# Value products spread over the projection, and page transfers in another order, in a one-core decoder step

## The reference

```python
h = _rmsnorm(x, pre_w)
z = h @ w_in                                  # 2048 -> 6980 columns
qa, ka, va, ga, qs, ks, vs, gs, qi, ki, wi = _split_cols(z)
# group A: differential attention, 8 heads
pr = softmax(s1) - lam * softmax(s2)
oa = einsum('bhqs,bshd->bqhd', pr, va_all)    # sample rows: 32 pages of keys and values each
# group B: the 256 best keys of each row by an indexer score
_, idx = lax.top_k(score, topk)
x = x + _rmsnorm(concat(oa, ob) @ w_out, post_w)
x = x + sigmoid(x @ w_pg + b_pg) * (p @ w_pe)
```

## Time and profile before

| | us |
|---|---|
| median of 3 runs | 3952.08 |
| lowest, highest | 3949.98, 3962.9 |
| the profiled execution, its own time | 3954.57 |
| its span in the trace | 3952.8 |
| TensorE busy in the span | 3453.9 (87%) |
| mean granted TensorE clock | 0.927 of full |
| DMA, mean over the span | 126 GB/s |

### The profile page before, as it was taken

One profiled execution on the slowest core, in us unless ns is written; L12 is line 12 of the kernel. 1 busy time (PEld: TensorE's weight loads), 2 busy tenths in 40 slices (PEclk: granted clock), 3 DMA queues, 4 the chain that ended last, 5 costly groups with the idle time before them and its releaser, 6 DMA issues. The chain is left out here.

```text
span 3952.8 us, 46957 instructions
## 1 busy us (share of the span) xinstructions
PE 3453.9 (87%) x16995; PEld 2339.6 (59%) x17025; DVE 1497.0 (38%) x2771; ACT 820.3 (21%) x1798; POOL 514.0 (13%) x480
## 2 busy tenths in 40 slices
PE   4969789898988888889358699999979999899999
PEld 3757567676766666667223677777744444444443
DVE  2028666666666676654555111111110002311111
ACT  4011424141423333221000122222220001110000
POOL 0004333333333232310000200000000000000000
PEclk9989899998999999999669699999989999999999
DMA  9864676666666766754100211111041101310110
GB/s 341 253 192 145 189 259 195 226 213 223 222 224 217 226 224 200 242 163 135 53 0 9 77 27 28 27 28 27 10 156 43 43 22 53 113 59 32 59 59 22
DMA packets 344067, 497.51 MB, mean 126 GB/s; under 512 B 58913, under 2 KB 244538, under 8 KB 342674
## 3 DMA queue, kind: packets, MB, share of 16 engines
q1 hardware_dynamic: 338384, 481.67, 38.3%
q10 hardware_dynamic: 3922, 8.65, 0.6%
q0 software_dynamic: 1536, 4.20, 0.4%
HBM read 466.55 MB, written 27.90 MB: 125 GB/s over the span
## 5 line engine op out<-in xcount | busy, mean ns | idle before, releaser
L1244 PE MATMUL Z<-W,hT 128*128 128x256 f32 x4608 | 1063.8, 389 | 37.7 <-ACT qk L829 24.1
L1244 PEld LDWEIGHTS Z<-W,hT 128*128 128x128 f32 x4608 | 887.7, 196 | 165.3 <-ACT qk L829 26.5
L2138 PE MATMUL S<-W,hT 128*128 128x512 f32 x1408 | 646.1, 597 | 8.1 <-DMA hT<-oT_d 8.1
L2138 PEld LDWEIGHTS S<-W,hT 128*128 128x128 f32 x1408 | 264.9, 191 | 356.0 <-issue 346.9
L800 POOL TENSOR_TENSOR kprod<-kib,qib 128x256 f32<-128x256 f32 x256 | 231.5, 908 | 696.8 <-DVE srel L965 554.2
L962 DVE TENSOR_REDUCE sc<-big 128x16 f32<-128x1024 f32 x256 | 309.7, 1210 | 0.5 <-DVE isc L999 0.3
L2138 PE MATMUL Z<-W,hT 128*128 128x512 f32 x640 | 303.6, 592 | 0.0
L794 POOL TENSOR_TENSOR big<-big,qb 128x1024 f32<-128x1024 f32 x96 | 231.9, 2416 | 274.6 <-DMA big<-in_cache_diff_k_dram 274.6
L1316 PE MATMUL DB<-big,ex 128*4 128x256 f32 (+1 forms) x2112 | 150.7, 397 | 109.1 <-DMA big<-in_cache_diff_v_dram 108.9
L958 DVE TENSOR_TENSOR big<-big,qb 128x1024 f32<-128x1024 f32 x160 | 197.6, 1235 | 126.4 <-DMA big<-in_cache_diff_k_dram 123.5
L2138 PEld LDWEIGHTS Z<-W,hT 128*128 128x128 f32 x640 | 121.5, 190 | 153.0 <-issue 152.6
(11 more groups left out here) (539 smaller groups left out, 3305.5 us busy)
## 6 DMA issues: line engine op xcount, KB each, us to landing
big<-in_cache_diff_k_dram SPq DMA_DIRECT2D x256, 512.0 KB, 5.5
big<-in_cache_diff_v_dram SPq DMA_DIRECT2D x256, 512.0 KB, 5.0
W<-in_w_in_dram SPq DMA_DIRECT2D x27, 2048.0 KB, 10.0
W<-in_w_in_dram SPq DMA_DIRECT2D x52, 1024.0 KB, 7.3
W<-in_w_ple_gate_dram SPq DMA_DIRECT2D x16, 1024.0 KB, 5.1
W<-in_w_out_dram SPq DMA_DIRECT2D x12, 1024.0 KB, 5.1
kib<-in_cache_idx_k_dram SPq DMA_DIRECT2D x256, 32.0 KB, 2.3
hT<-oT_d SPq DMA_DIRECT2D x3, 2048.0 KB, 21.5
```

Of the source, the lines that this page charges most:

```text
L1244: mm = pe.matmul(Z[b][:, 0:CW], hT[:, k, t * P:(t + 1) * P], W[:, w, k, :], start=(k == 0), stop=(k == KT - 1))
L2138: mm = pe.matmul(b, hT[:, k, t * P:(t + 1) * P], Wr[:, k, :], start=(k == 0), stop=(k == KT - 1))
```

## The change

The value products get four positions per place instead of three, with one page behind each half and two at the end of a place. The transfers of a slot are sorted by the place at which a table expects their home to be free (`key_done`, `value_done`); weights and the store of the keys are inserted where the table passes 4.1 and 5.6. The two rounds of slot 0 move to slot 8, where `settle` moves to place 3 and each `select` two places later, the last two behind place 7. `turned(0)` moves ahead of `take(0, 15)`. The values' store of the last slot has a semaphore of its own, and `stage` waits for an earlier store.

```diff
-        VALUES = ((0, 0, 0), (0, 0, 4), (2, 0, 3), (2, 0, 3), (0, 2, 3), (0, 2, 3), (0, 2, 3), (0, 2, 1))
-        ROUNDS_IN = (2,) + (4,) * (HA - 1) + (1,)
+        VALUES = ((0, 0, 0, 0), (0, 0, 0, 2)) + ((1, 1, 1, 2),) * 6
+        key_done = lambda s: [t + (0.35 if n == 0 else 0.5 + 0.5 * n / PAGES[s][t]) for t in range(NT) for n in range(PAGES[s][t])]
+        value_done = [t + 0.25 * (q + 1) for t in range(NT) for q in range(4) for n in range(VALUES[t][q])]
+        def transfers(s):
+            keys = [(u, 0, p + 4) for p, u in enumerate(key_done(s)) if p + 4 < NPG] if s < HA else []
+            vals = [(u, 1, v + 3) for v, u in enumerate(value_done) if v + 3 <= NPG] if s else []
+            return sorted(keys + vals)
+        ROUNDS_IN = (0,) + (4,) * (HA - 1) + (3,)
...
-                    for i in range(NPG):
-                        if s < HA:
-                            if i % 4 == 0 and i + 4 < NPG:
-                                index_pages(s, i // 4 + 1)
-                            if i + 4 < NPG:
-                                key_page(s, i + 4)
-                        if s and i + 3 <= NPG:
-                            value_page(s - 1, i + 3)
-                        if i == 18 and s + 1 < SLOTS:
-                            weights(s + 1, 0)
-                        if i == 25:
-                            store_keys(s)
+                    due = [(4.1, lambda: weights(s + 1, 0))] if s + 1 < SLOTS else []
+                    due.append((5.6, lambda: store_keys(s)))
+                    for u, kind, n in transfers(s):
+                        while due and due[0][0] < u:
+                            due.pop(0)[1]()
+                        if kind == 0:
+                            if n % 4 == 0:
+                                index_pages(s, n // 4)
+                            key_page(s, n)
+                        else:
+                            value_page(s - 1, n)
+                    for _, late in due:
+                        late()
...
 def stage(s, f):   # ScalarE
+                    act.wait_ge(st_v, 16 * (h + 1))
...
 for c in range(2 * NT):   # ScalarE, slot 0
+                    if c == 2 * NT - 1:
+                        turned(0)
                     take(0, c)
...
-                    if c >= 2 * NT - ROUNDS_IN[0]:
-                        counts(0, c - 2 * NT + ROUNDS_IN[0])
-                turned(0)
...
-                for r in range(ROUNDS_IN[0]):   # VectorE
-                    update(r)
...
-                            if t == 1:
+                            if t == 3:
                                 settle()
-                            if t >= 2:
-                                select(t)
+                            if t >= 4:
+                                select(t - 2)
                             if t == NT - 1:
+                                select(NT - 2)
+                                select(NT - 1)
                                 dve.nop().then_inc(d_sel, 1)
...
 half(s, 2 * t, 0)   # TensorE
+                        v = some(s, v, VALUES[t][0])
 half(s, 2 * t, 1)
...
-                        for n in range(pre):
-                            values(s, v + n)
+                        v = some(s, v, VALUES[t][1])
...
-                            for n in range(mid):
-                                values(s, v + n)
+                        v = some(s, v, VALUES[t][2])   # at t >= 4 behind probabilities(s, t, 0)
...
-                        for n in range(post):
-                            values(s, v + n)
+                        v = some(s, v, VALUES[t][3])   # behind output(s, t)
```

More of the change, by code:

```diff
@@ L575, in hymba_step @@
         PAGES.update({s: (0, 5, 5, 6, 4, 4, 5, 3) for s in range(1, HA)})
-        VALUES = ((0, 0, 0), (0, 0, 4), (2, 0, 3), (2, 0, 3), (0, 2, 3), (0, 2, 3), (0, 2, 3), (0, 2, 1))
-        ROUNDS_IN = (2,) + (4,) * (HA - 1) + (1,)
+        VALUES = ((0, 0, 0, 0), (0, 0, 0, 2)) + ((1, 1, 1, 2),) * 6
+        assert sum(map(sum, VALUES)) == NPG
+        key_done = lambda s: [t + (0.35 if n == 0 else 0.5 + 0.5 * n / PAGES[s][t]) for t in range(NT) for n in range(PAGES[s][t])]
[5 more added lines that the diff above has]
+        ROUNDS_IN = (0,) + (4,) * (HA - 1) + (3,)
         FIRST_ROUND = [sum(ROUNDS_IN[:s]) for s in range(SLOTS + 1)]
@@ L661, in hymba_step @@
         d_sel = sem("a_dsel")
-        st_k, st_v, st_o = sem("a_stk"), sem("a_stv"), sem("a_sto")
+        st_k, st_v, st_sv, st_o = sem("a_stk"), sem("a_stv"), sem("a_stsv"), sem("a_sto")
         with nc.Block() as block:
@@ L726, in store_values @@
                             sp.dma_start(sv_p.rearrange("l b (t p) h d -> p (l b t) h d", p=P)[:, :, n, :],
-                                         vg[:, s % 2, n, :, :]).then_inc(st_v, 16)
+                                         vg[:, s % 2, n, :, :]).then_inc(st_sv, 16)
                 sp.dma_start(subw[:, :], sub_w.partition_broadcast(P).rearrange("q l d -> q (l d)")).then_inc(x_in, 16)
@@ L760, in _ @@
                         sp.dma_start(sc[0:1, NPG, :], snew_a_d[s:s + 1, :]).then_inc(row_in, 16)
-                    for i in range(NPG):
-                        if s < HA:
-                            if i % 4 == 0 and i + 4 < NPG:
-                                index_pages(s, i // 4 + 1)
-                            if i + 4 < NPG:
-                                key_page(s, i + 4)
-                        if s and i + 3 <= NPG:
-                            value_page(s - 1, i + 3)
-                        if i == 18 and s + 1 < SLOTS:
-                            weights(s + 1, 0)
-                        if i == 25:
-                            store_keys(s)
+                    due = [(4.1, lambda: weights(s + 1, 0))] if s + 1 < SLOTS else []
[11 more added lines that the diff above has]
+                        late()
                 store_values(SLOTS - 1)
                 sp.wait_ge(st_k, 16 * SLOTS)
-                sp.wait_ge(st_v, 16 * (SLOTS + 1))
+                sp.wait_ge(st_v, 16 * HA)
+                sp.wait_ge(st_sv, 16 * HKV)
             @block.gpsimd
@@ L1321, in values, with some @@
                         pe.nop().then_inc(db_full, 1)
+                def some(s, v, n):
+                    for q in range(n):
+                        values(s, v + q)
+                    return v + n
                 def columns(s):
@@ L1339, in _ @@
                     for t in range(NT):
-                        pre, mid, post = VALUES[t]
                         scores(s, t)
@@ L1350, in _ @@
                             pe.transpose(DB[0:16, 256:384], m16, ident[:, :]).then_inc(db_full, 1)
-                        for n in range(pre):
-                            values(s, v + n)
-                        v += pre
+                        v = some(s, v, VALUES[t][1])
                         if t < 4:
@@ L1369, in _ @@
                             probabilities(s, t, 0)
-                            for n in range(mid):
-                                values(s, v + n)
-                            v += mid
+                        v = some(s, v, VALUES[t][2])
+                        if t >= 4:
                             probabilities(s, t, 1)
@@ L1379, in _ @@
                         output(s, t)
-                        for n in range(post):
-                            values(s, v + n)
-                        v += post
+                        v = some(s, v, VALUES[t][3])
                     values(s, NPG)
```

## The result

The changed kernel takes 4013.01 us (median of 4 runs, 4009.94 to 4021.68) against 3951.67 for the kernel before on the same chip: a ratio of 1.0153, 95% interval 1.0128 to 1.0177. It is slower, by 61 us where 26.5 were forecast, and lies above the range (3890 to 4005). In the profiled execution the span is 4008.1 us, 55.3 more than before.

A forecast was written before the change was run, and what follows sets the result against it. TensorE, in order, bounds the kernel with its waits. Slots 2 to 7 add 14.5 us, the slot 0 to 1 boundary 0 and slot 8 12: +26.5 on 3954.6, less 2.5 to the median, gives 3978.6 us; range 3890 to 4005.

The forecast's parts named there:

- The waits in a slot: Slots 2 to 7: six TensorE waits in places 2 to 6, 23.0 us in all.
- the key page waiting into the next place holds the value pages: Places 4, 5 and 6: a key transfer held until the next place's `maxima` delays value pages; waits 3.2, 2.5, 3.5 us.
- the walk: One slot followed place by place at full clock; in place 2 V3 follows four indexer pages and K8, wait 4.2 us.
- the weights only move their stall: End of place 4: weights, indexer pages and K20 delay V16, wait 5.2 us; the old stall moves and doesn't go.
- Clock: Slots 2 to 7: each of six waits loses 1.7 us by slow clock, 10.2 us a slot.
- Spreading them moves no work; it can only move waits: Value products in every slot: still 33 at 0.5 us each, so spreading them adds no TensorE time.
- The slot without waits: Slots 2 to 7: 156.7 us, from slot 8's 162.0 less its value-page waits and about 1 us of slow clock.
- Slot 0 to 1: Boundary and slot 1: the 23.3 us idle gap goes but later waits use it up; net 0, bounds -16 and +5.
- Slot 8: Last slot: value waits and clock save 6 us, ScalarE's wait costs 4.4 + 1.7, which cancels; its end adds 12 us.
- the tail: End of slot 8: three selects follow place 7's `combine`, so `turned(8)` starts later; +12 us, bounds +9 and +14.
- the case's own bounds: Whole kernel: the forecast case's own range, 3935 to 4010 us.
- The cheap rivals: Whole kernel: SP's issues hold up nothing, about 3846 us, chance 0.13; all value waits go, about 3800 us, chance 0.06.

The follow-up runs named there:

- last_key: The changed kernel with only each place's last key page taken as free later (t + 1.3 instead of about t + 0.9): 3878.74 us.
- weights_late: The changed kernel with the next slot's weights at 5.3 instead of 4.1 in the order of transfers: 4020.33 us.
- key_take5: The changed kernel with key homes taken as free one page later and ScalarE emptying half 5's bank before its counts in place 2: 3821.97 us.
- spread_only: The kernel before with the value products at the change's positions, transfers and rounds as before: 3877.35 us.
- key_next: The changed kernel with the table taking a key page's home as free when the next page is processed: 3851.17 us.
- the shifted table: The changed kernel with key homes taken as free when the next page is processed: 3851.17 us; with the old product groups too, 4013.11 us.

## Why the prediction was wrong

Sign, places and mechanism of the waits were right; the size wasn't, because one term that had been put at zero isn't zero. By the prediction's own steps:

- **The waits in a slot** were to be 4.2, 4.4, 3.2, 5.2, 2.5 and 3.5, in all 23.0. Over slots 2 to 7 they measured on average 4.6, 4.5, 2.3, 4.5, 2.8 and 3.4, in all 22.1, each at its product; small ones at product 12 add 0.5. Single terms were off by up to 0.9, and part of the good sum is errors that cancel. That the key page waiting into the next place holds the value pages is shown by last_key together with SP's rows (above for place 4; the same pattern stands in places 5 and 6). In place 2 it was mostly the indexer pages ahead of K8, as the walk had it. That the weights only move their stall is shown by weights_late.
- **Clock**: 1.7 per wait, 10.2 in all. TensorE is busy for 169.8 us a slot on average; with the same products at a granted clock of 1.00 (key_take5) it is busy for 159.3. That is 10.5. Right.
- **"Spreading them moves no work; it can only move waits"** is the step that failed. The slot without waits was put at 156.7 and measures 160.1 (15.9, 16.7, 20.0, 19.6, 20.5, 21.0, 21.6, 24.8): each product alone breaks the row of halves. The term was zero and is +3.4 a slot, over seven slots some 24 of the missing 29 us of the trace (55.3 against 26.5); the rest is small terms, such as 2 us in the later stages and slot 8's clock. The row it was taken from, three products in 1.48 us, shows a product inside a group, not one alone. (The spreading itself costs nearer 4 us, as 156.7 was about 1 us too long: slot 8 took 161.7 us, not 162.0, and its clock of 0.989 is some 1.8 us lost, not 1.) The second half of the sentence fails too: with the old transfers the spread products cut TensorE's waits from 21.0 to 10.2 us a slot (spread_only).
- **Trace and median**: the medians are 61 us apart and the traces 55, since the profiled execution of the kernel before was 2.9 us above its median and that of the changed kernel 3.1 below. So 6 us of the miss in the median come from which execution was profiled.
- **Slot 0 to 1**: net 0; slot 2 starts at 612.3 against 611.6. TensorE's first wait moved as walked:

```profile
423.87 0.38 PE L1367 MATMUL DB<-ident,small 128*16 128x128 f32 x1 [7.38 <-DVE small L1148]
...
471.90 1.03 PE L1327 MATMUL DB<-big,ex 128*4 128x256 f32 x8 [12.07 <-DMA big<-in_cache_diff_v_dram]
```

  The 23.3 us of the earlier trace rows came back as 7.4 and 12.1. V3 went at 467.40, where 466.5 was forecast.
- **Slot 8**: the tail was to be +12 from the start of place 7. It is 54.0 us from there to the next stage against 41.9, +12.1, and the copies of `turned(8)` start at 1949.06, 32.3 us into the place (compare). But the forecast had the rest of the slot at zero, and it is +3.7 up to place 7: again the spread products, and a clock of 0.98. For ScalarE's wait 1.7 us of clock was put, and place 3 lost 2.9.
- **The range**: the case's own bounds ended at 4010, the stated range at 4005, and the measured 4013 lies outside both. The missing term wasn't in them, as the cost of a product was taken as known. The cheap rivals (3846, 3800) had a chance of 0.19 between them. Neither holds for this order. That key_next came out at 3851, near the first of them, doesn't bear that rival out: SP's issues cost the same there, and only the order differs.

## What to carry to other kernels

When transfers are sorted by the time at which a home comes free, take that time from the instruction that signals it. Here pages were freed one step after they were touched, and on an in-order queue one such page per place (one of them with four indexer pages) cost 134 us, more than the 79 us that spreading the work had gained. Small transfers belong in the count of the queue's time, and a stall of the queue isn't cured by moving what causes it to another place that is just as tight: here the stall moved along. And spreading short products between long ones isn't free: read the price from a row where one stands alone.

## What the runs showed that was not expected

- The order and the grouping act on each other far more than they add. The new groups alone give -79 us. With the rounds moved as well (+7 by themselves), the shifted table gives +58 with the old groups and -105 with the new ones, and the unshifted table gives +61 with the new ones.
- The slow clock goes with the longer waits. With waits of at most 1.9 us slots 2 to 7 of key_take5 ran at a granted clock of 1.00. In the changed kernel one wait of 4.5 went with 0.98 in slot 8, and six of 2.6 to 5.0 with 0.93 in slot 3. The length of a wait doesn't decide alone, though: in slot 7 of spread_only a wait of 1.92 us ended at 1609.6, and at 1611.0 the granted clock fell to 0.50.
